# A depthwise convolution split over three engines beside eight attention heads

## What is computed

```python
z = h @ w_in[l]
q_a = apply_axial_rope(rms_norm(q_a, q_norm[l]))          # 8 heads of 64
k_a = apply_axial_rope(rms_norm(k_a, k_norm[l]))          # 2 key heads
o_att = block_attention(q_a, k_a, v_a)                    # softmax(q k^T / 8) v
o_hg = hgrn2_bidirectional(...)                           # gated recurrence, 4 heads

u = a_c * sigmoid(g_c)                                    # conformer_conv, 256 channels
y = depthwise_conv(u, w_dw)                               # 31 taps over the tokens
y = layer_norm(y + b_dw, ln_g, ln_b)                      # over the channels
o_cv = silu(y)

x = x + concatenate([o_att, o_hg, o_cv]) @ w_out[l]
```

## Time and profile before

| | us |
|---|---|
| three runs: lowest, median, highest | 2791.85, 2794.12, 2797.46 |
| the profiled execution | 2793.34 |
| its span | 2791.1 |
| mixing stage of layer 0, from the last in-projection matmul to the out-projection | 109.9 to 178.8 |
| the same in layer 1 | 491.4 to 558.0 |

### The profile page before, as it was taken

How to read it: one execution, slowest core, us unless ns; L and a number is a source line. 1 busy time by engine, 2 the same in 40 slices (tenths; PEclk the granted TensorE clock), 3 DMA queues, 4 the chain that set the end, 5 groups by cost and what they waited for, 6 DMA issues and landing times.

```text
span 2791.1 us, 45655 instructions
## 1 busy us (share of the span) xinstructions
PE 2716.9 (97%) x18588; PEld 2472.1 (89%) x18588; DVE 1701.7 (61%) x2680; ACT 1369.1 (49%) x1713; POOL 135.7 (5%) x68
## 2 busy tenths in 40 slices
PE   8999999899999999999999999999999999999997
PEld 8869889699897999999999888987999999999886
DVE  5546546456456699745555566566899645545565
ACT  5445443554345468734444444444568644444442
POOL 0000000000000600000000000001500000000000
PEclk9999999999999999999999999999999999999999
DMA  5215552055535436755565675523356756565672
GB/s 214 106 61 198 184 213 106 33 185 181 196 129 187 165 138 215 283 214 208 211 213 208 214 275 202 185 93 138 137 180 233 270 197 223 197 222 204 230 261 88
DMA packets 74410, 515.97 MB, mean 185 GB/s; under 512 B 8273, under 2 KB 8545, under 8 KB 18593
## 3 DMA queue, kind: packets, MB, share of 16 engines
q1 hardware_dynamic: 58576, 424.70, 42.8%
q0 software_dynamic: 10208, 43.45, 4.6%
q10 hardware_dynamic: 5488, 45.91, 4.0%
HBM read 474.19 MB, written 39.85 MB: 184 GB/s over the span
## 4 chain that ended last, share of the span: by engine, by line
PE 89%; DVE 9%; ACT 1%; issue 1%; DMA 1%; ACTq 0%; DVEq 0%
PE lin L1552 17%; PE lin L1554 17%; PE lin L1553 17%; PE m L1553 8%; PE m L1554 8%; PE m L1552 8%; PE m L2082 4%; PE lin L1727 2%; DVE lo L936 1%; PE m L1671 1%; PE m L1692 1%; PE m L2061 0%; PE m L1981 0%; PE m L1800 0%; PE m L1704 0%
## 5 line engine op out<-in xcount | busy, mean ns | idle before, releaser
L936 DVE TENSOR_TENSOR lo<-raw,hi 128x2048 fp32r<-128x2048 f32 x357 | 816.0, 2291 | 673.7 <-ACT hi L442 672.6
L442 ACT ACTIVATE hi<-raw 128x2048 fp32r<-128x2048 f32 x403 | 768.7, 1910 | 487.3 <-PE m L1554 346.6
L1552 PE MATMUL lin<-xh,hi 128*128 128x256 f32 x3376 | 974.2, 289 | 12.9 <-DVE lo L936 5.6
L1553 PE MATMUL lin<-xl,hi 128*128 128x256 f32 x3376 | 955.9, 283 | 0.0
L1554 PE MATMUL lin<-xh,lo 128*128 128x256 f32 x3376 | 955.5, 283 | 0.0
L1552 PEld LDWEIGHTS lin<-xh,hi 128*128 128x128 f32 x3376 | 645.9, 191 | 22.0 <-DVE lo L936 6.8
L1553 PEld LDWEIGHTS lin<-xl,hi 128*128 128x128 f32 x3376 | 646.7, 192 | 3.7 <-issue 1.0
L1554 PEld LDWEIGHTS lin<-xh,lo 128*128 128x128 f32 x3376 | 646.2, 191 | 0.0
L1554 PE MATMUL m<-hi,al 128*128 128x512 f32 x1024 | 401.9, 393 | 0.0
L1553 PE MATMUL m<-lo,ah 128*128 128x512 f32 x1024 | 401.9, 392 | 0.0
L1552 PE MATMUL m<-hi,ah 128*128 128x512 f32 x1024 | 398.7, 389 | 0.0
(11 more groups left out here) (350 smaller groups left out, 2816.0 us busy)
## 6 DMA issues: line engine op xcount, KB each, us to landing
raw<-stream SPq DMA_DIRECT2D x403, 1024.0 KB, 4.8
gate_table<-stg ACTq DMA_DIRECT2D x16, 2048.0 KB, 10.7
g<-gate_table POOLq DMA_DIRECT2D x32, 1024.0 KB, 8.6
rows<-rows ACTq DMA_DIRECT2D x4, 1024.0 KB, 7.1
memh<-mem_turned_scratch POOLq DMA_DIRECT2D x3, 1024.0 KB, 5.1
meml<-mem_turned_scratch POOLq DMA_DIRECT2D x3, 1024.0 KB, 9.6
x_scratch<-x ACTq DMA_DIRECT2D x2, 1024.0 KB, 4.2
x<-x_scratch ACTq DMA_DIRECT2D x2, 1024.0 KB, 6.1
```

Source lines behind the costliest of these rows:

```text
L442: act.activation(HI[i % SLOTS][:], RAW[:, i % SLOTS, :], ACT.Copy).then_inc(hi_ready, 1)
L936: dve.tensor_tensor(LO[i % SLOTS][:], RAW[:, i % SLOTS, :], HI[i % SLOTS][:].bitcast(F32), ALU.subtract).then_inc(lo_ready, 1)
L1552: pe.matmul(out_, ah, bh, start=first, stop=False, **kw)
L1553: pe.matmul(out_, ah, bl, start=False, stop=False, **kw)
```

## The change

The 31 taps of channel tile 1 leave TensorE. For each of them ScalarE multiplies the shifted input by the weights (`products`, a 128x256 copy with a scale per partition). The results go in turn to four buffers: the halves of `EG` and `AC`, free at that time. GpSimd adds them up in `W[:, 256:512]` (`add_products`), each add waiting for the one before; ScalarE may be four products ahead. The bias now waits for the last tap and the last add. `TAPS_AT` holds 31 taps. On VectorE the scaling of head n + 1 is put ahead of round n's side work, and the maximum of head n + 3 behind it. TensorE gets `keep_warm`: 8 and 6 matmuls of constants, per layer, into unused columns, ahead of the turns of heads 0 and 2; their result is never read.

```diff
-TAPS_AT = [6, 6, 8, 6] + [9] * 4
+TAPS_AT = [4, 4, 5, 4, 4, 4, 3, 3]
...
+        def tap_product(i):
+            return (EG, AC)[i % 4 // 2][:, 256 * (i % 2):256 * (i % 2) + 256]
...
+                def products(n0, n1):
+                    act.wait_ge(sem("up_ready"), l + 1)
+                    for i in range(n0, n1):
+                        if i >= 4:
+                            act.wait_ge(sem("tap_added"), CONV_K * l + i - 3)
+                        a.mark(act.activation(tap_product(i), UP[:, 1, i:i + TOK], ACT.Copy, scale=par(l, "cw", CONV_K + i)), sem("tap_made"))
...
-                diags(DIAGS, taps[3])
+                products(0, 4)
+                diags(DIAGS, taps[4])
+                products(4, 8)
                 a.step(act.activation(SCN[:], GT[:], ACT.Exp, scale=-1.0))
                 sigmoid(SCN[:], sem("scn_ready"))
-                diags(taps[3], taps[4])
+                products(8, 12)
...
                 def more_diags(n):
                     if n < 2:
-                        diags(taps[4 + 2 * n], taps[6 + 2 * n])
+                        for i in range(taps[4 + 2 * n], taps[6 + 2 * n]):
+                            diags(i, i + 1)
+                            p = 12 + 8 * n + i - taps[4 + 2 * n]
+                            products(p, p + 1)
+                        products(p + 1, 20 if n == 0 else CONV_K)
...
             head_max(0)
             head_max(1)
+            head_scale(0)
+            head_max(2)
             for n in range(8):
-                head_scale(n)
-                if n + 2 < 8:
-                    head_max(n + 2)
+                if n + 1 < 8:
+                    head_scale(n + 1)
                 between(n)
+                if n + 3 < 8:
+                    head_max(n + 3)
...
-                        dve.wait_ge(sem("diag_used"), 2 * CONV_K * (l + 1))
-                        for ct in range(2):
+                        dve.wait_ge(sem("diag_used"), CONV_K * (l + 1))
+                        dve.wait_ge(sem("tap_added"), CONV_K * (l + 1))
+                        for ct, sums in enumerate((PS[1][:, 0:256], W[:, 256:512])):
...
+            def add_products(l):
+                sums = W[:, 256:512]
+                for i in range(CONV_K):
+                    n = CONV_K * l + i
+                    pool.wait_ge(sem("tap_made"), n + 1)
+                    if i == 0:
+                        ins = pool.tensor_copy(sums, tap_product(i))
+                    else:
+                        pool.wait_ge(sem("tap_added"), n)
+                        ins = pool.tensor_tensor(sums, sums, tap_product(i), ALU.add)
+                    ins.then_inc(sem("tap_added"), 1)
...
+                def keep_warm(n):
+                    for _ in range(n):
+                        pe.matmul(PS[1][:, 256:512], cst("ident"), CST[:, 0:256], start=False, stop=False, skip_group_check=True)
...
                 taps(3)
+                keep_warm(8)
                 turn(0)
                 for n in range(8):
                     g, o = 8 * l + n, 64 * (n // 4)
+                    if n == 1:
+                        keep_warm(6)
```

More of the change, by code:

```diff
@@ L1095, in other_outputs @@
                     elif n == 2:
[L1096 to L1097 removed]
+                        dve.wait_ge(sem("diag_used"), CONV_K * (l + 1))
+                        dve.wait_ge(sem("tap_added"), CONV_K * (l + 1))
+                        for ct, sums in enumerate((PS[1][:, 0:256], W[:, 256:512])):
                             c = slice(256 * ct, 256 * ct + 256)
[L1099 removed]
+                            v.step(dve.tensor_scalar(AC[:, c], sums, par(l, "cb", ct), None, ALU.add), sem("cy0_ready"))
                     elif n == 3:
@@ L1510, in _ @@
                 elif g == 2:
+                    add_products(1)
                     pool.wait_ge(sem("mixl_ready"), 3)
```

9 lines of the change are left out of this document (4 added, 5 removed).

## The result

The changed kernel takes **2778.6 us** (median of 3 runs, 2778.5 to 2780.4) against 2794.1 us before. The ratio is 0.9942, with a 95% interval from 0.9928 to 0.9955. Run again beside the experiments, it took 2781.0 us (0.9949, 0.9936 to 0.9962). The forecast was 2778.0.

A forecast was written before the change was run, and what follows sets the result against it. TensorE, busy for 97% of the span, was taken as the bound. Bias add (2.8 and 1.2 us) and relay (6.3 and 5.7 us) sum to 16.0 us, giving 2778.1 us against the median of 2794.12; range 2766 to 2794.

The forecast's parts named there:

- Taps, front of the stage: 31 of 62 taps a layer leave TensorE, 14.0 us of its work; layer 0's first turn could start at 128.0.
- ScalarE: Convolution products in ScalarE's queue, 0.36 us each; ScalarE alone would let layer 0's bias start at 144.2.
- Add on GpSimd: Each of 31 serial adds a layer taken as 0.85 us, between 0.58 and 1.11; 26.4 us in all.
- rival C: Slower serial GpSimd adds, ScalarE blocked for product buffers; decides from 1.11 us an add, 2806 at 1.3; chance 0.10.
- Holds between VectorE and GpSimd: Shared port: VectorE's operations before the bias add hold GpSimd's adds for their full duration, 10.9 us in layer 0.
- 139.3 plus holds: End of GpSimd's adds in layer 0: 139.3 unheld, 150.2 with holds, so the bias starts 2.8 us sooner.
- Relay: Head steps from bias add to out-projection: 19.4 us instead of 25.8 and 25.1, gaining 6.3 and 5.7 us.
- Sum: Gains of both layers' bias adds and relays: 2.8 + 6.3 + 1.2 + 5.7 = 16.0 us.
- the gain should stay: Behind the stages comes TensorE's own work with its next weights already split, so the 16.0 us should be kept.
- A: Ports don't block for two SBUF inputs, adds at the short end, ScalarE sets the bias: 2768 us; chance 0.17.
- B: GpSimd loads code before layer 0's first add, about 6 us once, which makes 2784 us; chance 0.24.
- D: Gains given back as TensorE idles and its clock halves; relay as long as now, gain 4.0, 2790 us; chance 0.07.

The follow-up runs named there:

- e1: Changed kernel without the eight and six constant products ahead of the first and third turns: 2782.7 us, ratio 0.9956.
- e6: Changed kernel with VectorE's two subtractions moved behind the second head's scale: 2779.6 us, ratio 0.9947.
- e2: Kernel before with VectorE's new order alone, scaling a head's weights one step sooner: 2785.0 us, ratio 0.9966.
- e3: Changed kernel with VectorE's old order of maxima and scales, keeping the split and constant products: 2795.6 us, ratio 0.9997.

## Why the prediction was right, point by point

The time was right to 0.6 us, and that close it was by luck. Some steps held; in the sum two errors cancelled ahead of the bias add, and behind the sum two more: the stages gained 3.2 us more than forecast and the second block lost 4.8. The runs of one kernel also spread by more than 0.6 us.

- **Taps, front of the stage.** The first turn was put at 128.0 us and came at 128.27, for another reason. The working had the weights ready at 127.0 and the constant products as the later ones, at a cost of 1.0 us. Measured, the products end near 127.7 and TensorE waits 0.56 us more for the weights: VectorE's two subtractions took 5.43 instead of 4.50 us and the scaling 1.11 instead of 0.62, both beside GpSimd's adds. So the eight constant products cost nothing, and e1 shows it.
- **ScalarE.** A product was put at 0.36 us; back to back its start-to-start time is 0.40 us (0.50 us long, overlapping the next by 0.10), as in this row of two. ScalarE's last product ended at 145.3 us, with the bias bound at 144.2 in the working.

```profile
119.34 0.90 ACT L524 ACTIVATE eg<-up,pr 128x256 f32<-128x256 f32 x2
```

- **Add on GpSimd.** Taken as 0.85 us between 0.58 and 1.11; measured 0.87. This decides rival C, which needed 1.11: it didn't come true.
- **Holds between VectorE and GpSimd.** Put at 10.9 us, each operation of VectorE at its full duration. Adding up what exceeds 1.74 us from pair to pair, the adds were held for 5.8 us: 4.8 beside the two subtractions and the rotation's sum ahead of them, 1.0 beside all short ones. The rule named there (the Trainium skill, SBUF — State Buffer, "Who interferes with whom") is borne out for long operations: 4.8 us of holds beside the 6.0 us that they take alone. With short ones, VectorE is the one that waits (0.62 becomes 1.02, 0.69 becomes 1.10), and costs GpSimd little. The upper bound was taken for all; for the short ones the lower was near.
- **A wait that the working lacks.** The working treated ScalarE's line (144.2) and GpSimd's (139.3 plus holds) as two lines, and took the later one. But GpSimd's thirteenth add needs a product behind the first head's copy in ScalarE's queue. The adds restart at 131.23, and from there 18 steps of 0.87 and the 1.0 of small holds lead to the last one at 147.86. In all GpSimd waits 4.0 us for ScalarE, which was put at nothing. With 5.8 instead of 10.9 of holds, the two errors nearly cancel: bias add at 148.72 against 150.2 forecast, which is luck. That the wait counts, e6 shows: with the long holds mostly gone the wait is 6.10 us and the bias add doesn't move.
- **Relay.** Put at 19.4 us for both layers; measured 19.42 and 18.76. Its steps: turn 4 at 3.9 us after the bias add where 2.9 stood, then turns 3.6 us apart, measured 4.4, 3.6 and 2.7 (the last was 2.7 in the working as well), and 4.9 to the end where 4.6 stood. The first two are long in the stretch from 149 to 155 us where the clock is 0.72, behind TensorE's wait for the bias add: the product ahead of turn 4 takes 1.97 us there and 1.08 later. The 2.0 us kept for half clock were right in size.
- **Its cause.** The prediction gave the whole relay gain to VectorE's order. By e2 that is so for 5.6 us of 6.3. But it also took the bias add's gain for a gain of the program by itself. By e3 the bias add comes just as soon in the old order, and the relay behind it is 3.3 us longer than in the kernel before, so that nearly all of it is lost again. The gain reaches the end only together with the order.
- **Sum.** 16.0 us forecast, 19.2 gained in the two stages (layer 0: 4.0 and 6.3 against 2.8 and 6.3; layer 1: 2.7 and 6.3 against 1.2 and 5.7).
- **The steps that failed** are the sentence behind the sum, "the gain should stay", and ScalarE's line taken as apart from GpSimd's. Against the first, 4.8 us were lost in the second block, with the clock at its lower level in unchanged code; why it falls in this kernel stays open. Without this the time would have been near 2774, an estimate from 2778.6 less 4.8, still in the range.
- **Rivals.** A (no blocking) fell with the 4.52 us pair. B (code loading of 6 us, as the page GPSIMD Engine Reference of the Trainium skill, "Instruction dispatch", has it) fell: between the first copy and the first add GpSimd is idle for 0.15 us. D (half clock eats the gain) fell for the change, but is much what happens to the split in the old order: the relay is 29.0 us at 0.50 and 0.60.

## What to carry to other kernels

When work leaves the engine that is last for a chain of small steps over other engines, follow each link through the queue of the engine that makes it: a chain restarts behind whatever stands ahead of its next operand, and a saving ahead of such a place is lost. An engine that loses work ahead of a relay may only gain waits, and with them a lower clock, as here in e3, so look at what it will wait for next before taking work off it. And compare stage by stage before crediting an edit with a gain: here some 4 to 5 us of a median lie in a stretch that no edit touched.

## What the runs showed of the hardware

- GpSimd: a 128x256 float32 add takes 0.72 us, 0.87 us from start to start in a chain in which each waits for the one before; a copy of that size 0.40 us. Between the copy and the first add GpSimd is idle for 0.15 us, so no loading time shows there.
- VectorE and GpSimd hold each other up (a pair of adds takes 4.52 and 3.46 us beside the subtractions, 1.59 alone), also where VectorE has one SBUF input beside per-partition scalars: two head scalings take 1.02 us beside adds and 0.61 alone. The Trainium skill, SBUF — State Buffer, "Who interferes with whom", names this operation among those that can take the shared port pair; the runs agree. By the same section the maximum is free of this, and it is: 0.69 us in both kernels.
- ScalarE's scaled copy of 128x256 takes 0.50 us and every 0.40 us one can start, with adds and subtractions beside it too (0.90 us for the two at 119.34).
- TensorE's clock: behind one and the same wait of 1.98 us it fell to the lower level for several us in four traces and stayed at the upper one in others, and the runs put this at 4 to 8 us. Elsewhere a wait of 3.35 us was followed by 0.50 and 0.60 over the 16 us behind it (e3), one of 1.75 us by 0.72 over 6 us (the changed kernel). The length of the wait alone doesn't decide it: in the kernel before, layer 1, TensorE waited 2.72 us ahead of 552.75, and the clock was 1.00 from 552 to 557 us.
